# The final norm of a MoE decoder step done under the 32nd expert, with that expert's own rows normed again by gather and scatter

## What is computed

```python
x = x + concat([ya, yb]) @ w_out                     # mixer, residual
h2 = rmsnorm(x, norm2_g)
eidx, gates = hier_route(h2, ...)                    # 2 experts of 32 for each token
x = x + sum over the token's 2 experts e of gate * (silu(h2 @ w1[e]) * (h2 @ w3[e])) @ w2[e]
y = x * rsqrt(mean(x * x, axis=-1) + EPS) * normf_g  # y_prompt, y_sample
```

## Time and profile before

| what | value |
|---|---|
| median of three executions | 964.62 us |
| profiled execution, its own time | 957.51 us |
| span of the profiled execution | 955.7 us |
| PE busy (matmul) | 883.1 us, 92% of the span |
| DVE, ACT, POOL busy | 280.4, 102.9, 155.6 us |
| last matmul to the end | 919.8 to 955.7 us |

### The profile page before, as it was taken

How to read it: one execution, slowest core, us unless ns; L and a number is a source line. 1 busy time by engine, 2 the same in 40 slices (tenths; PEclk the granted TensorE clock), 3 DMA queues, 4 the chain that set the end, 5 groups by cost and what they waited for, 6 DMA issues and landing times. The chain is left out here.

```text
span 955.7 us, 28225 instructions
## 1 busy us (share of the span) xinstructions
PE 883.1 (92%) x12202; PEld 637.1 (67%) x12202; DVE 280.4 (29%) x839; ACT 102.9 (11%) x159; POOL 155.6 (16%) x262
## 2 busy tenths in 40 slices
PE   5899999999999997899999999999999799999940
PEld 2757758576684854867768686868686576767620
DVE  2544656547465454350010101010101001010106
ACT  1110110101011013001001010101010010100003
POOL 1000100000000011212212222222222122223110
PEclk9999999999999997799999999999999999999985
DMA  8780200201021029699999999999999999999948
GB/s 335 242 311 1 90 23 22 88 0 44 0 88 45 3 90 340 241 397 402 392 394 408 389 410 387 409 389 407 389 408 388 408 401 395 406 393 400 399 152 320
DMA packets 57390, 258.10 MB, mean 270 GB/s; under 512 B 10643, under 2 KB 11723, under 8 KB 40436
## 3 DMA queue, kind: packets, MB, share of 16 engines
q1 hardware_dynamic: 47436, 237.98, 61.9%
q0 software_dynamic: 9264, 19.32, 8.1%
q10 hardware_dynamic: 640, 0.07, 0.1%
HBM read 240.33 MB, written 25.04 MB: 278 GB/s over the span
## 5 line engine op out<-in xcount | busy, mean ns | idle before, releaser
L1413 PEld LDWEIGHTS ps<-hT,big 128*64 128x64 f32 x8192 | 292.4, 139 | 36.1 <-issue 34.7
L1413 PE MATMUL ps<-hT,big 128*64 128x80 f32 (+2 forms) x8192 | 297.8, 235 | 11.8 <-issue 10.7
L1434 PE MATMUL ps<-big,poolT 128*80 128x512 f32 (+2 forms) x512 | 191.4, 594 | 1.0 <-issue 0.6
L1167 DVE TENSOR_TENSOR poolT<-u,ps 128x320 f32<-128x320 f32 (+2 forms) x32 | 15.5, 486 | 405.1 <-PE ps L1413 405.1
L1434 PEld LDWEIGHTS ps<-big,poolT 128*80 128x80 f32 (+2 forms) x512 | 64.3, 149 | 103.9 <-issue 101.6
L1285 PEld LDWEIGHTS ps<-hT,big 128*64 128x64 f32 x2048 | 111.5, 137 | 7.0 <-issue 6.1
L1285 PE MATMUL ps<-hT,big 128*64 128x128 f32 x2048 | 115.3, 273 | 0.0
L591 POOL DMA_INDIRECT x_rows<-xn,sidx x22 | 32.9, 1496 | 263.3 <-ACT xn L799 253.1
L568 POOL DMA_INDIRECT slot_table<-ids,dest x18 | 18.7, 1037 | 302.7 <-DVE dest L916 300.0
L1272 PE MATMUL ps<-big,hT 128*128 128x512 f32 x128 | 59.8, 620 | 3.0 <-DMA big<-in_w_in 1.6
L1354 PE MATMUL ps<-big 128*128 128x512 f32 x128 | 56.9, 598 | 1.5 <-DVE big L1037 1.5
(11 more groups left out here) (205 smaller groups left out, 573.3 us busy)
## 6 DMA issues: line engine op xcount, KB each, us to landing
big<-in_exp_w SPq DMA_DIRECT2D x192, 1024.0 KB, 23.4
big<-in_w_in SPq DMA_DIRECT2D x4, 1536.0 KB, 12.8
big<-in_w_out SPq DMA_DIRECT2D x2, 2048.0 KB, 17.8
x_rows<-big SPq DMA_DIRECT2D x8, 512.0 KB, 2.6
h_rows<-xn SPq DMA_DIRECT2D x8, 512.0 KB, 2.9
big<-x_rows SPq DMA_DIRECT2D x8, 512.0 KB, 6.9
out_y_prompt<-big SPq DMA_DIRECT2D x8, 512.0 KB, 2.8
big<-in_x_prompt SPq DMA_DIRECT2D x1, 3072.0 KB, 11.2
```

What stands on the lines that cost most here:

```text
L1413: last = pe.matmul(out[c * w:(c + 1) * w, j, 0:m], up_weights(n)[:, k, j * P + c * w:j * P + (c + 1) * w], xT[:, 4 * half + k, 0:m], start ...
L1434: last = pe.matmul(ps[first:first + m, 5 + cols, :], hhT[:, 2 * half + k, 0:m], down_weights(n)[:, k, cols * 512:(cols + 1) * 512], start= ...
```

## The change

`FREE = 31` blocks are what the nine tiles now wait for. SP loads them once blocks 0 to 30 have landed in `x3_rows` and PE has used all their weights, while block 31 still runs; they are squared, normed and stored as before. POOL holds back the scatter of block 31 until all nine loads have landed, so that the tiles hold none of its rows. After that scatter has landed, POOL gathers block 31's up to 64 rows from `x3_rows` into `xg[1]`; ACT and DVE norm these rows (`norm_late`); and when all nine tiles have been stored, POOL scatters them over the outputs (`scatter_out`, one DMA for `y_prompt`, one for `y_sample`; an index outside an output is skipped). Tiles 7 and 8 (`HANDED = 2`) are multiplied by 1/rms on ACT and by `gf` on POOL. The groups of `norm_tiles` are now 0-1, 2-4 and 5-8. If an expert overflows, everything is loaded and normed a second time; that branch is not taken here.

The core of the diff:

```diff
+HANDED = 2
+TILE_GROUPS = (range(0, 2), range(2, 5), range(5, NT))
+FREE = 31
+LATE = NE - FREE
@@ sync, behind the weights @@
+            def load_rows():
+                for j in range(NT):
+                    m = P if j < LAST else NS
+                    sp.dma_start(x3[j][0:m, :], x3_rows[P * j:P * j + m, :]).then_inc(x3_in[j], 16)
+            def store_rows(turn):
+                for j in range(NT):
+                    if j < NT - HANDED:
+                        sp.wait_ge(y_out, turn * (NT - HANDED) + j + 1)
+                    else:
+                        sp.wait_ge(xn_ready, NT + turn * HANDED + j - (NT - HANDED) + 1)
...
+                    sp.dma_start(dst, x3[j][0:m, :]).then_inc(y_stored, 16)
+            for s in range(SETS):
+                sp.wait_ge(rows_out[s], 16 * len(range(s, FREE, SETS)))
+            sp.wait_ge(used, CH * FREE)
+            load_rows()
+            store_rows(0)
             sp.wait_ge(plan_ready, 1)
...
+            sp.wait_ge(y_stored, 16 * NT)
+            for s in range(len(FINAL_CAPS) - LATE, len(FINAL_CAPS)):
+                sp.wait_ge(rows_out[s], 16 * (FINAL + 1 + 2))
...
-            for s in range(SETS):
-                sp.wait_ge(rows_out[s], 16 * len(range(s, NE, SETS)))
-            sp.wait_ge(ov_free, over + 1)
@@ gpsimd @@
+            def scale_handed(turn):
+                pool.wait_ge(ssf_set, 2)
+                for n, j in enumerate(range(NT - HANDED, NT)):
+                    m = P if j < LAST else NS
+                    pool.wait_ge(xq_made, 2 + turn * HANDED + n + 1)
+                    pool.tensor_tensor(x3[j][0:m, :], x3[j][0:m, :], gf[0:m, :], ALU.mult).then_inc(xn_ready, 1)
@@ gpsimd, block_triple @@
+                    if isinstance(b, int) and b >= FREE:
+                        for j in range(NT):
+                            pool.wait_ge(x3_in[j], 16)
                     pool.wait_ge(y_ready, count)
                     scatter_add(ys[s][0:m, :], sidx[s][0:m, :], rows_out[s])
+                    if isinstance(b, int) and b >= FREE:
+                        pool.wait_ge(xgT_done, NE)
+                        pool.wait_ge(rows_out[s], h * 16 + 16)
+                        gather_sum(xg[s][0:m, :], sidx[s][0:m, :], rows_in[s])
@@ gpsimd, behind the blocks @@
+            scale_handed(0)
+            pool.wait_ge(numbered, 3 + LATE)
+            pool.wait_ge(x2n_ready, NT + 1)
+            pool.wait_ge(y_stored, 16 * NT)
...
+            scatter_out(xg[1][0:FINAL_CAPS[1], :], sidx[1][0:FINAL_CAPS[1], :], gidx[1][0:FINAL_CAPS[1], :], rows_out[1])
@@ scalar, block_triple @@
                     act.activation(s1T[:, :, 0:m], up1[:, :, 0:m], ACT.Silu).then_inc(silu_done, 1)
+                    if isinstance(b, int) and b == NE - 1:
+                        square_tiles(range(0, 2))
                     act.wait_ge(used, b * CH + CH)
@@ scalar, behind the blocks @@
+            def scale_handed(turn):
+                act.wait_ge(rs3, (turn + 1) * len(TILE_GROUPS))
+                for j in range(NT - HANDED, NT):
+                    m = P if j < LAST else NS
+                    act.activation(x3[j][0:m, :], x3[j][0:m, :], ACT.Copy, scale=ssf[0:m, 1, j:j + 1])\
+                        .then_inc(xq_made, 1)
+            square_tiles(range(2, NT))
+            scale_handed(0)
...
+            act.wait_ge(rows_in[1], 16 * (FINAL + 2))
+            m = FINAL_CAPS[1]
+            act.activation(junk[0:m, :], xg[1][0:m, :], ACT.Square, accum_out=ss2[0:m, 0:1]).then_inc(sq2, 1)
@@ vector @@
+                    if isinstance(b, int) and b == FINAL * SETS:
+                        dve.memset(ssf[:, :, :], 1.0).then_inc(ssf_set, 1)
+                        dve.wait_ge(in_gf, 16)
+                        dve.tensor_scalar(gf[:, :], gf[:, :], NEWTON, None, ALU.mult).then_inc(ssf_set, 1)
@@ vector, behind the blocks @@
+            for n, tiles in enumerate(TILE_GROUPS):
+                norm_tiles(n, tiles)
+            norm_late(1, ss2, sq2, rs2_step, rs2, x2n_ready)
```

More of the change, by code:

```diff
@@ L511, in _ @@
                         sp.dma_start(chunk_dst(c, c), chunk_src(e, c)).then_inc(ov_w, 16)
-            for s in range(SETS):
-                sp.wait_ge(rows_out[s], 16 * len(range(s, NE, SETS)))
-            sp.wait_ge(ov_free, over + 1)
[L517 to L525, removed]
+                sp.wait_ge(ov_free, over + 1)
+                load_rows()
+                store_rows(1)
+                sp.wait_ge(y_stored, 16 * 2 * NT)
         @block.gpsimd
@@ L690, in _ @@
                     pool.memset(gidx[0][:, :], 0).then_inc(ov_free, 1)
+                scale_handed(1)
         @block.scalar
@@ L784, in _, with square_tiles @@
                           gates.rearrange("p j c -> p (j c)")).then_inc(gates_stored, 16)
+            def square_tiles(tiles, turn=0):
+                for j in tiles:
+                    m = P if j < LAST else NS
+                    act.wait_ge(x3_in[j], 16 * turn + 16)
+                    reached(act, sq3, turn * NT + j)
+                    if turn + j == 0:
+                        act.wait_ge(ssf_set, 2)
+                    act.activation(junk[0:m, :], x3[j][0:m, :], ACT.Square,
+                                   accum_out=ssf[0:m, 0, j:j + 1]).then_inc(sq3, 1)
             def block_triple(h, caps_of):
@@ L812, in _ @@
                                    scale=gslot[0][:, 0:1]).then_inc(ov_y, 1)
[L814 to L821, removed]
+                square_tiles(range(NT), 1)
+                scale_handed(1)
         @block.vector
@@ L1160, in plan_overflow, with norm_tiles, norm_late @@
                     plan_step, 0, plan_ready)
+            def norm_tiles(turn, tiles, past=0):
+                dve.wait_ge(sq3, past + tiles[-1] + 1)
+                w = ssf[:, :, tiles[0]:tiles[-1] + 1]
+                rstd(w, w[:, 0:1], 1.0 / D, rs3_step, turn, rs3, several=True)
+                dve.wait_ge(rs3, turn + 1)
+                for j in tiles:
+                    if j >= NT - HANDED:
+                        break
+                    m = P if j < LAST else NS
+                    dve.scalar_tensor_tensor(x3[j][0:m, :], x3[j][0:m, :], ssf[0:m, 1, j:j + 1],
+                                             gf[0:m, :], ALU.mult, ALU.mult).then_inc(y_out, 1)
+            def norm_late(s, w, squares, step, rs, ready):
+                m = FINAL_CAPS[s]
+                dve.wait_ge(sidx_ready, FINAL * SETS + s + 1)
+                dve.wait_ge(rows_in[s], 16 * (FINAL + 2))
+                dve.tensor_scalar(gidx[s][0:m, :], sidx[s][0:m, :], SEQ, None, ALU.bitwise_xor).then_inc(numbered, 1)
+                dve.wait_ge(squares, NT + 1)
+                rstd(w[0:m, :], w[0:m, 0:1], 1.0 / D, step, NT, rs)
+                dve.wait_ge(rs, NT + 1)
+                dve.scalar_tensor_tensor(xg[s][0:m, :], xg[s][0:m, :], w[0:m, 1:2], gf[0:m, :],
+                                         ALU.mult, ALU.mult).then_inc(ready, 1)
             def block_triple(h, caps_of):
@@ L1164, in block_triple @@
                     b = h * SETS + s
+                    if isinstance(b, int) and b == FINAL * SETS:
+                        dve.memset(ssf[:, :, :], 1.0).then_inc(ssf_set, 1)
+                        dve.wait_ge(in_gf, 16)
+                        dve.tensor_scalar(gf[:, :], gf[:, :], NEWTON, None, ALU.mult).then_inc(ssf_set, 1)
+                        dve.wait_ge(ssf_set, 2)
                     dve.wait_ge(silu_done, b + 1)
@@ L1193, in _ @@
                         .then_inc(ov_h, 1)
[L1196 to L1199, removed]
-                dve.wait_ge(rs3, turn + 1)
-                for j in tiles:
-                    m = P if j < LAST else NS
-                    dve.scalar_tensor_tensor(x3[j][0:m, :], x3[j][0:m, :], ssf[0:m, 1, j:j + 1],
-                                             gf[0:m, :], ALU.mult, ALU.mult).then_inc(y_out, 1)
-            dve.memset(ssf[:, :, :], 1.0).then_inc(ssf_set, 1)
-            dve.wait_ge(in_gf, 16)
-            dve.tensor_scalar(gf[:, :], gf[:, :], NEWTON, None, ALU.mult).then_inc(ssf_set, 1)
-            dve.wait_ge(ssf_set, 2)
-            for turn, tiles in enumerate((range(0, 3), range(3, 6), range(6, NT))):
-                norm_tiles(turn, tiles)
+                for n, tiles in enumerate(TILE_GROUPS):
+                    norm_tiles(len(TILE_GROUPS) + n, tiles, NT)
         @block.tensor
```

24 lines of the change are left out of this document (22 added, 2 removed).

## The result

The changed kernel is slower by 0.7%: 972.49 us (median of nine, 968.88 to 976.83) against 966.12 us (nine of the kernel before, 961.88 to 969.64), ratio 1.0071, 95% interval 1.0044 to 1.0098. The forecast was 4.1 us less than before, a ratio of 0.9957. The profiled execution of after took 971.17 us, with a span of 969.2.

A forecast was written before the change was run, and what follows sets the result against it. PE's expert work fills nearly all the span; the change touches the unoverlapped 35.9 us end. Span = 941.25 + S + G, 951.6 against 955.7, so 964.62 - 4.1 = 960.5 us; range 957.5 to 967.5.

The forecast's parts named there:

- S: POOL's chain at the end: time for block 31's scatter to land, taken as 6.0 us beside queued tile stores.
- G: POOL's chain at the end: time for the gather of block 31's rows to land, taken as 4.3 us.
- The loads' start: SP's tile loads wait only for block 30's scatter, landing in 7.8 us: issued at 915.8, 11.3 us earlier.
- Rival 2: Quiet transfers in POOL's chain: S = 4.8, G = 4.1, stores missing POOL's DMAs; 959.0 us; chance 0.16.
- rival 3: Contended transfers in POOL's chain: tile stores slow its DMAs, S = 8.4, G = 9.1; 967.7 us; chance 0.24.
- Rival 4: POOL's multiplies of the handed tiles end last, 2.8 us a tile or held up by DVE; 961.7 us; chance 0.10.
- The 2.2 a tile: POOL's multiplies of the two handed tiles: 2.2 us each, ending at 943.1.
- The output scatters: POOL's last two DMAs: first issued at 947.1, landing in 4.1 us; second at 948.3, landing in 2.7.
- The end: After the output scatters land at 951.2, a closing 0.4 us gives a span of 951.6.
- the 11.3 won at the start: Loads issued 11.3 us earlier; 9.3 of it goes back at once to block 31's scatter waiting for tile 8.

The follow-up runs named there:

- the kernel with the three mends: Changed kernel plus an early POOL drain behind block 31's gate gather, HANDED = 0, and POOL leaving without awaiting its output scatters; 0.9984 times before.

## Why the prediction was wrong

Offsets are from the end of the last matmul, by the forecast (919.8) and in after (927.7).

| step of the forecast | forecast | measured |
|---|---|---|
| first load issued | -4.0 | -5.25 |
| block 31's scatter issued | +11.0 | +11.25 |
| S, its landing | 6.0 | 6.5 |
| gather issued | +17.9 | +18.5 |
| G, its landing | 4.3 | 3.8 |
| second multiply of POOL done | +23.3 | +24.1 |
| its store, of tile 8, landed | +26.3 | +27.0 |
| gathered rows ready | +26.35 | +26.5 |
| first output scatter issued | +27.3 | +27.9 |
| output scatters landed | +31.4 | +31.4 |
| end of the span | +31.8 | +41.5 |

**The loads' start** was right in kind and off by 1.25 us, early: block 30's scatter was issued at -10.4 instead of -11.9, but landed after 5.2 us (917.26 to 922.43) instead of the 7.8. The nine loads then took longer: tile 8 was in at +15.6 from the first issue (938.95 less 0.9, against 922.45) instead of +14.1. Why isn't known. It wasn't the weights: from 922 to 924 us no packets but the loads' and 7 small ones of POOL's queue moved. The tile stores are at most a part of it: tile 3 was already about 1 us late when squared (931.35, +8.9 against +7.9 in before), ahead of the first store at 931.98. The two errors cancel by luck, and the scatter is 0.25 off.

**S and G** were estimated one by one as 6.0 and 4.3 and came to 6.5 (938.95 to 945.43, the gather's issue less 0.75) and 3.8 (946.18 to 950.00). Their sum is 10.3, as forecast, again because two errors cancel. Rival 2 (8.9) and rival 3 (17.5) fall. Rival 4 is half right: the path through POOL's multiplies and tile 8's store did end last, 0.5 us behind the gathered rows, because POOL came to them 0.6 later than forecast; but not by 2.8 a tile, and undoing it changed nothing that the times show. The 2.2 a tile was 2.32. The estimate by the Trainium skill's page on GpSimd was 2.25, from "GPSIMD Engine Reference", section "Performance versus the Vector engine"; the trace agrees.

**The output scatters** were issued 0.6 late, and landed on the forecast time only because they were quicker: 3.2 us for the first, forecast at 4.1, and 2.3 for the second, forecast at 2.7.

**The end** is the step that failed, in the sentence "With the closing 0.4 the span is 951.6". The 0.4 was read from the kernel before, between SP's last wait and the end, and taken for a constant of the program. It was the time of whichever engine is last, and that was SP. When POOL is last it is 10.0 (959.16 to 969.2): its memset, the 9.63 of the drain, the barrier. The difference, 9.6, is all but 0.1 of the 9.7 by which the tail exceeds the forecast's 31.8. Both signs are shown: putting POOL's end last in the kernel before costs 9.1 us of tail, and paying the drain early in the changed kernel gives 9.0 back. The row with its price was in the trace of before, at the barrier's own line, 9,382 ns starting at 927.2. The forecast asked of every edit what would hide its cost, and didn't ask it of what each engine does after its last instruction.

Rival 3 had the right sign for a reason that did not occur, so it isn't confirmed by the result.

**What remains of the change** without the drain is small, as forecast: 0.9991 and 0.9984 for the two kernels with an early drain, where the forecast's 960.5 against 964.62 is 0.9957. The first one's tail of 32.5 is 3.4 us shorter than before's; the ratios' intervals (0.9962 to 1.0019 and 0.9963 to 1.0004) don't tell the gain from nothing, and lie a little above the forecast ratio. That most of the 11.3 won at the start is given back at the scatter stands in after's own trace, where block 31's scatter is issued at +11.25, 9.5 later than the +1.8 of before; the version that gathers first has no such scatter and gains 0.66%.

## What to carry to other kernels

Read what stands at the closing barrier's line for every engine, not only for the one that ends now: a change that makes another engine the last one exposes that engine's drain, and GpSimd's closing one is 9.4 to 10.8 us in this program when none has gone shortly before. If GpSimd must be last, let it drain once while it waits for something else anyway. And when a step is moved ahead only to wait behind another (here a scatter that may not touch what is being loaded), ask whether the dependence can be met in SBUF in place of HBM. Here the early loads with the scatter's wait gained nothing that could be measured, and the same loads without it gained 0.66%.

## What the runs showed of the hardware

- POOL's drain at the end of its program took 9.38 us (before), 9.63 (after) and 10.44 (32 more gathers spread over the blocks), and 0.38 when an earlier drain of 9.30 had gone before. Right behind the issue of a gather, beside the nine loads, a drain took 12.5 to 13.0. It is not busy time, and DMAs issued by SP go on beside it.
- An indirect DMA's issue on POOL is longer beside DVE's multiplies of two SBUF inputs: the gather took 0.99 us in after, with DVE idle, and 1.85 in the kernel without handed tiles, where it started at 944.46 and DVE multiplied until 945.43; from there to the issue's end it is 0.9 again. In the kernel with the three mends it is the same (1.84, and 0.9 from DVE's end at 949.87). Block 31's scatter took 1.60 in before, with DVE idle, and 2.01 in after, where DVE multiplied for its first 0.7.
- A gather of 64 rows landed in 3.8 us with only the last stores under way (after), in 5.2 when its issue was held up beside DVE, and in 7.9 beside the nine loads; a scatter-add of 64 rows in 6.5 beside the tile stores, between the 4.8 and 7.8 of the earlier trace rows.
